# GpSimd's subtraction of a weight piece: four instructions of 512 columns in place of one of 2048

## What is computed

```python
f = swiglu(rmsnorm(h, pre_g), w_gate, w_up, w_down)      # 1024 -> 2816 -> 1024
h = h + 0.5 * rmsnorm(f, post_g)
m = hybrid_mixer(rmsnorm(h, mix_pre_g), w_in, ...)       # gates * attentions, then @ w_out
h = h + rmsnorm(m, mix_post_g)
f = swiglu(rmsnorm(h, ...), ...); h = h + 0.5 * rmsnorm(f, ...)
# second block
conv_out = conv_module(u_val, u_gate, conv_w, ...)       # 31 taps over time, per channel
attn = forgetting_attention(q, k, v, f_logit)
x = x + g1 * ((sigmoid(gate_c) * conv_out + sigmoid(gate_a) * (attn @ w_attn_out)) @ w_out)
x = x + g2 * moe_ffn(h2, ...)
```

## Time and profile before

| what | value |
|---|---|
| median of three runs | 2073.63 us |
| lowest, highest run | 2070.16, 2073.76 us |
| span of the profiled execution | 2071.4 us |
| its own device time | not listed apart from the three runs |
| mean granted clock of TensorE | 0.955 of full speed |
| GpSimd's subtractions | 110, median 4610 ns, 520.3 us in all |

### The profile page before, as it was taken

One profiled execution on the slowest core, in us unless ns is written; L12 is line 12 of the kernel. 1 busy time (PEld: TensorE's weight loads), 2 busy tenths in 40 slices (PEclk: granted clock), 3 DMA queues, 4 the chain that ended last, 5 costly groups with the idle time before them and its releaser, 6 DMA issues.

```text
span 2071.4 us, 29205 instructions
## 1 busy us (share of the span) xinstructions
PE 1936.2 (93%) x10964; PEld 1194.4 (58%) x10965; DVE 862.1 (42%) x1424; ACT 506.7 (24%) x830; POOL 520.5 (25%) x114
## 2 busy tenths in 40 slices
PE   6878889899989998987889999999999999999997
PEld 6877888667889997876753333333333333333333
DVE  5889620225159902998532222222222222212223
ACT  4222343443243345333421001100110001001101
POOL 5566646022058884533500000000000000000000
PEclk8999999999999999887879999999999999999999
DMA  7666634212435553421359999999999999999793
GB/s 276 246 248 256 223 121 163 79 44 82 142 106 188 188 186 105 143 82 61 128 208 398 418 418 417 419 417 417 418 418 418 417 419 418 417 418 418 295 419 152
DMA packets 98648, 559.55 MB, mean 270 GB/s; under 512 B 8960, under 2 KB 11136, under 8 KB 50304
## 3 DMA queue, kind: packets, MB, share of 16 engines
q1 hardware_dynamic: 98400, 558.30, 68.8%
q10 hardware_dynamic: 192, 0.46, 0.1%
HBM read 557.68 MB, written 1.05 MB: 270 GB/s over the span
## 4 chain that ended last, share of the span: by engine, by line
PE 65%; DVE 20%; DMA 7%; issue 4%; ACT 3%; DVEq 0%; POOL 0%; SPq 0%; ACTq 0%
PE bank L1048 20%; PE bank L1113 10%; DVE arena L1525 7%; DVE hid_hi L1605 6%; DMA ring<-w_exp_in 5%; PE bank L580 5%; PE bank L582 4%; PE bank L581 4%; PE bank L662 3%; PE bank L1059 3%; PE bank L1032 3%; PE bank L1079 3%; PE bank L574 2%; DMA arena<-ada 2%; PE bank L1104 2%
## 5 line engine op out<-in xcount | busy, mean ns | idle before, releaser
L1492 POOL TENSOR_TENSOR w_lo<-ring,w_hi 128x2048 fp32r<-128x2048 f32 x110 | 520.3, 4733 | 514.3 <-ACT w_hi L1171 514.2
L1048 PE MATMUL bank<-ring,arena 128*64 128x512 f32 x2112 | 470.7, 597 | 2.0 <-DMA ring<-w_exp_in 2.0
L580 PE MATMUL bank<-x_hi,w_hi 128*128 128x256 f32 (+1 forms) x1272 | 384.2, 302 | 51.0 <-DVE arena L1600 32.6
L581 PE MATMUL bank<-x_lo,w_hi 128*128 128x256 f32 (+1 forms) x1272 | 377.1, 296 | 0.0
L582 PE MATMUL bank<-x_hi,w_lo 128*128 128x256 f32 (+1 forms) x1272 | 376.8, 296 | 0.0
L1048 PEld LDWEIGHTS bank<-ring,arena 128*64 128x64 f32 x2112 | 145.8, 137 | 307.3 <-issue 297.6
L580 PEld LDWEIGHTS bank<-x_hi,w_hi 128*128 128x128 f32 x1272 | 256.2, 201 | 68.4 <-issue 48.6
L582 PEld LDWEIGHTS bank<-x_hi,w_lo 128*128 128x128 f32 x1272 | 257.1, 202 | 0.0
L581 PEld LDWEIGHTS bank<-x_lo,w_hi 128*128 128x128 f32 x1272 | 256.6, 202 | 0.0
L1113 PE MATMUL bank<-ring,arena 128*64 128x512 f32 x1056 | 233.9, 595 | 0.0
L1171 ACT ACTIVATE w_hi<-ring 128x2048 fp32r<-128x2048 f32 x110 | 210.1, 1910 | 92.8 <-PE bank L580 92.5
(11 more groups left out here) (278 smaller groups left out, 1980.4 us busy)
## 6 DMA issues: line engine op xcount, KB each, us to landing
ring<-w_exp_in SPq DMA_DIRECT2D x256, 1024.0 KB, 16.7
ring<-w_exp_out SPq DMA_DIRECT2D x128, 1024.0 KB, 16.1
ring<-stream SPq DMA_DIRECT2D x120, 1024.0 KB, 4.9
arena<-ada SPq DMA_DIRECT2D x48, 512.0 KB, 4.4
cst<-const_in SPq DMA_DIRECT2D x1, 1568.0 KB, 19.9
res<-xT_in SPq DMA_DIRECT2D x1, 1088.0 KB, 6.2
outT<-arena SPq DMA_DIRECT2D x2, 512.0 KB, 3.0
arena<-c_in SPq DMA_DIRECT2D x1, 512.0 KB, 11.2
```

Of the source, the lines that this page charges most:

```text
L580: begin = mm(out_, wh, xh, start=start, stop=False)
L581: mm(out_, wh, xl, start=False, stop=False)
L1048: last = mm(bank[2 + gu][pr, :], xT[:, k % 4, k // 4, :], ring[:, k, c0:c0 + 512], start=False, stop=(k == KD - 1), tile_position=pos)
L1492: nc.gpsimd.tensor_tensor(w_lo[:, BUF[p], :], ring[:, p % RING, :], w_hi[:, BUF[p], :].bitcast(f32), ALU.subtract).then_inc(w_split, 1)
```

## The change

`rest` issues the subtraction as four instructions over 512 columns each, one behind the other, and each counts one on `w_split`. The three places at which TensorE waits for a piece count four for each piece. Nothing else is changed; w_lo gets the same values.

```diff
 PIECE = 2048
+REST_COLS = 512
+RESTS = PIECE // REST_COLS
...
-                    pe.wait_ge(w_split, piece)
+                    pe.wait_ge(w_split, piece * RESTS)
...
-                            pe.wait_ge(w_split, ORDER[at] + p + 1)
+                            pe.wait_ge(w_split, (ORDER[at] + p + 1) * RESTS)
...
-                            pe.wait_ge(w_split, ORDER[p] + 1)
+                            pe.wait_ge(w_split, (ORDER[p] + 1) * RESTS)
...
             def rest(p, n):
 
                 pool.wait_ge(w_high, n)
-                nc.gpsimd.tensor_tensor(w_lo[:, BUF[p], :], ring[:, p % RING, :], w_hi[:, BUF[p], :].bitcast(f32),
-                                        ALU.subtract).then_inc(w_split, 1)
+                for c in range(0, PIECE, REST_COLS):
+                    last = nc.gpsimd.tensor_tensor(w_lo[:, BUF[p], c:c + REST_COLS],
+                                                   ring[:, p % RING, c:c + REST_COLS],
+                                                   w_hi[:, BUF[p], c:c + REST_COLS].bitcast(f32), ALU.subtract)
+                    last.then_inc(w_split, 1)
```

## The result

| kernel | median (range) of runs | ratio to before |
|---|---|---|
| before | 2073.07 us (2070.16 to 2073.76, 4 runs) | 1 |
| changed | 2029.8 us (2023.05 to 2031.32, 4 runs) | 0.9783 [0.9766, 0.98] |

The changed kernel is 43 us faster. The profiled execution of the changed kernel took 2023.05 us, with a span of 2021.2; it is the fastest of the four, so the difference of the two spans, 50.2 us, holds some 6 us of scatter. One run of the kernel before, beside the first four experiments, took 9055.84 us in a slow state and is left out of every comparison.

The account below looks back on a forecast made before the run. Whole GpSimd subtractions and certain VectorE instructions exclude each other, costing VectorE 3.9 us a piece in the first FFN. Terms -3 + 0 + 1 + 1 - 8 = -9; 2071.4 - 9 + 2.2 = 2064.6, say 2065 us, range 2048 to 2083.

Parts of the forecast that it names:

- The price of an added instruction: On GpSimd, each instruction added to a piece was to cost 0.12 us, at least 0.03 and at most 0.46.
- Release between quarters: Between GpSimd's quarters VectorE is let in, so the second FFN's cast takes 1.0 to 1.4 us, not 4.4.
- Rival A: No release: the second quarter takes over before VectorE is let in; +8, 2081 us, slower; chance 0.17.
- Second FFN and down projection: TensorE is busy throughout there and the delay is hidden, so removing it brings nothing: 0.
- Rival B: GpSimd becomes the bound, in the second FFN's tile, if an added instruction costs near 0.35 us; +8, 2081 us; chance 0.15.
- Rival C: First FFN packs well, VectorE almost at the exclusion's floor: -16 of 22 there, -9 at output projection, 2049 us; chance 0.16.
- The excluded work is conserved by cutting it.: First FFN: 101 us of GpSimd and 70 of VectorE, 171 of 193 us, stay excluded; only overlap is gained.
- First FFN: From 29 to 222 us, more overlap under quarters: -3 us, between +9 and the most, 22 us gained.
- Convolution: VectorE's taps set the pace and lose the same 25 us in shorter waits; +1 us for handovers, bounds -4 and +6.
- Output projection: In the second mixer, the sum L1721 is done before TensorE asks, removing idle stretches: -8 us, bounds 0 and -10.
- First pieces: At the start of a mixer or FFN, TensorE waits for the first piece in about three places: +1 us.

Follow-up runs that it names:

- the first four experiments: Against the kernel before, pieces cut in four in the first FFN only, 2042.05 us; in the mixers only, 2056.25; everywhere in two, 2053.08; everywhere in eight, 2033.09.
- the uneven cut: Against the kernel before, every piece's subtraction cut into four instructions of 1664, 128, 128 and 128 columns; 2046.78 us, ratio 0.9872.

## Why the prediction was wrong in size

**The price of an added instruction** held: (5.03 - 4.61) / 3 = 0.14 us, where 5.03 is an undisturbed piece of four quarters; predicted 0.12.

**Release between quarters** held. Rival A fell: the longest cast of the changed kernel is 1.39 us, its median 790 ns against 4110.

**Second FFN and down projection** held, to within 1 us: full before and after. Rival B fell at this size; with eight cuts GpSimd does set the pace, but in the first FFN. (Rival C's 2049 us leaves out the two terms of +1; with them it would be 2051.)

**The step that failed** is the sentence "The excluded work is conserved by cutting it." The prediction saw that a tap loses 4.20 us to a piece of 4.66 and called the other 0.46 a possible price of each instruction. It did not ask what else this gap says: in 0.46 us of its span the piece excludes nothing, and if each added instruction has such ends while costing only 0.12 us, then each takes a few tenths off the excluded time. The measured line says 0.19 us for each. The spans of the six sizes give the same: they lie on 2.16 ns a column plus 0.18 us, so the ends that exclude nothing are 0.37 to 0.39 us in every size, and an added instruction gives them at 0.18 us of span. The prediction even took the whole piece's hidden 0.3 us as the reason to expect little, when four cuts hide it four times.

**First FFN.** Term -3, measured -28.7, beyond the bound of -22. The bound rested on 171 us of excluded work that cannot shrink. It shrank by 0.58 us a piece (4.23 less 3.65), 14 us over 24 pieces, close to the 15.6 that the uneven cut gives. The other 13.1 us are what the prediction had as overlap and took at a seventh of the most: waits that are cut short let VectorE's steps behind a tile (L1605 above all) come in time. That this is how they do it is argued from TensorE's shorter wait for L1605, not shown by a run of its own. The sum also had no term for the clock here, as it had at the output projection: TensorE's busy time fell by 9.5 us at 0.96 in place of 0.90. Rival C named this end (-16 there), for the reason of overlap alone.

**Convolution.** Term +1, bounds -4 and +6, measured -9.9. Here the failed step is bare. VectorE sets the pace, some 19 pieces are split in the stage, and each excludes 4.23 - 3.65 = 0.58 us less: 11 us, against 9.7 less of VectorE's busy time there. That this agrees so well is in part luck: the same sum for eight cuts, 19 x 1.3 = 25, falls short of the 31.5 measured; where the rest comes from, the runs do not tell.

**Output projection.** Term -8, measured -5.5 and -6.9 in two executions. The mechanism held: L1726 at 0.42 to 1.48 us, and TensorE's idle stretches of 2.7 us gone. The size was off because x_lo (L1580), right behind the sum, is now the one to wait, 1.1 us each time; the prediction followed only L1721. With eight cuts the stage gives 8.6 to 8.8.

**First pieces** (+1) can't be told from scatter.

Sum by stages of the profiled pair: -28.7 - 9.9 - 5.5 - 1 for the second FFN = -45.1, and the medians differ by 43.3.

## What to carry to other kernels

Where long instructions of GpSimd and certain ones of VectorE exclude each other, cut GpSimd's into several: it costs 0.14 us each and takes 0.19 us of exclusion away each, besides shortening the wait. Cut no further than until GpSimd itself has no idle time left, and set the number stage by stage: here four where a TensorE-bound FFN needs a piece each 5.7 us, eight where VectorE sets the pace. And if a row shows a gap between what an instruction takes and what it takes from others, ask of it both what it costs and what it gives when there are more of them.

## What the runs showed of the hardware

- An fp32 subtraction of n columns on GpSimd (128 partitions, two SBUF inputs) delays a VectorE instruction that it excludes by 2.155 ns x n - 0.19 us: 4.23, 3.41, 2.02, 0.91, 0.36 and 0.08 us for 2048, 1664, 1024, 512, 256 and 128 columns. Its own span in the median is 4.61, 3.78, 2.41, 1.30, 0.74 and 0.46 us. A piece with nothing of VectorE's between spans 4.61 us as one instruction, 4.75 as two, 5.03 as four and 5.61 as eight.
- The exclusion changes hands between two GpSimd instructions that stand back to back with no wait between them; a quarter and a tap then alternate, 1.43 us a pair, less than 1.30 + 0.48.
- TensorE's granted clock in the first FFN was 0.90 with 40.0 us of idle time in 193.0, 0.96 with 20.3 in 163.8, and 1.00 with 1.8 in 131.0 (29 to 160 us, three quarters of the subtraction left out).
- The Trainium skill (GPSIMD Engine Reference, section 2.1) says that consecutive Pool instructions are no barrier, from which the prediction had made rival A. The trace agrees that they overlap, a quarter starts 0.04 us before the one ahead of it ends, but they do not keep VectorE out: the cast's longest time fell to 1.39 us. From the floor of about 2.5 cycles an element that the Trainium skill gives in the same section, the prediction's estimate left 0.35 us for start and end; the spans of six sizes give 2.16 ns a column and 0.18 us, of which 0.04 lies under the instruction ahead.
